# A new hand-written order of calls where the mLSTM ends and attention and the output projection begin, in a two-layer hybrid encoder on one core

## The chip, the cores and the metric

The kernel runs on one core of one Trainium2 chip, in one launch. The metric is the time of the launch on the device in microseconds (us), and the runs shown are executions of the same program. TensorE is PE in the profile (PEld its weight loads), VectorE is DVE, ScalarE is ACT, GpSimd is POOL, SyncE is SP.

## The reference, cut to what matters

Two sequences, of 256 and of 1024 tokens with 1024 features, go through the same two layers, in float32.

```
h = rmsnorm(x)
aq ak av | sz sxbc sdt | mq mk mv mo mi mf = split(h @ w_in)
ya = window attention (4 query heads, 2 key heads, blocks of 128, neighbours on each side, a sink)
yb = bidirectional SSD scan, gated with silu(z), normed
yc = bidirectional mLSTM, normed, gated with sigmoid(o)
x  = x + concat(ya, yb, yc) @ w_out
x  = x + expert-choice mixture of 16 experts(rmsnorm(x))
```

The window attention of a block is `p = exp(s - m)`, divided by `sum(p) + exp(sink - m)`, times V.

## The kernel before

Both sequences lie side by side as NC = 10 chunks of 128 tokens: 0 and 1 are the short sequence, 2 to 9 the long one. A layer has stages: norm and transposes, input projection with the convolutions, SSD, mLSTM, attention with output projection, routing, and the experts. Attention and output projection take the chunks in the order 2 to 9, 0, 1, and a chunk's number n there is its place in this order. Layers are a loop, so each line runs twice.

Nothing plans the work at run time: each engine has its own list of calls, written out by hand, does them strictly in that order, and waits in front of a call until counters (semaphores) of other engines have come far enough. A call that waits holds up all that stands behind it on its engine. A helper adds one to its own engine's counter after each instruction and waits for it, so instructions of DVE, ACT and POOL run one by one. Because helpers record them, most rows carry a helper's line: L1472 is `mm` (any matmul), L976 a tensor_tensor of DVE, L980, L982 and L985 other forms of DVE. A float32 matmul is two instructions in the trace, a transpose one.

The calls that matter here, with n the chunk's place (of the mLSTM calls the chunk itself):

- PE: `ml_sum(9)` is the last product of the mLSTM. `turn_qk(n)` transposes normed queries and keys (3 transposes), `scores(n, j)` makes the scores of half the heads, `turn_p(n, h)` transposes the probabilities of head h, `turn_y(n, 0)`, `(n, 1)` transpose the outputs of SSD and mLSTM, and `turn_y(n, 2)` multiplies probabilities and V. `out_proj(n, hf, i0, i1)` does steps i0 to i1 of the 8 contraction steps of one half of the output columns; one step is 2 instructions of 512 columns. Steps 0 to 3 need `keep_y(n, 0)`, 4 and 5 `keep_y(n, 1)`, 6 and 7 `keep_y(n, 2)`.
- DVE: `ml_read(c)` takes the mLSTM sums from PSUM, `ml_output(c)` makes its output and the sums of squares (10 instructions, the last one lets POOL make the root), `ml_gate(c)` scales and gates it when POOL has made the root. `attn_square(n)` sums the squares of queries and keys. `keep_turned(n)` takes the result of `turn_qk(n)` from PSUM (counter `a_kept`). `attn_shift(n, j)` adds the bias to scores and takes the maximum; its second half (j = 1) releases ACT's exponentials. `attn_den(n)` makes one over the sum of the exponentials and releases `attn_scale(n)`. `keep_y(n, j)` takes the result of `turn_y(n, j)` from PSUM. `add_x` adds the residual, `take_x(0)` is the first of them.
- POOL: `rroot` is the root for a norm (2 instructions), `attn_root(n)` the same for queries and keys, `attn_norm(n)` scales queries and keys (2 instructions), `attn_scale(n)` divides all probabilities of a block.
- ACT: `attn_exps(0)`, `attn_exps(1)`, `keep_p(0)`, `keep_p(1)`, `attn_exps(2)`, in this order, then norm, `keep_p` and `attn_exps` of each next block. `keep_p(n)` copies what `turn_p(n, h)` left in PSUM.

The waits at the head of the calls that the change moves past each other:

```
turn_p(n, h):    pn_made >= n + 1          (attn_scale(n) done), p_kept two heads back
turn_y(n, 2):    p_kept >= 4 * (n + 1), yt_copied >= 3 * n + 2, and for n < 2 a_kept >= n + 4
scores(n, j):    a_kept >= turned_for(n), and for n >= 1 s_read >= 2 * n + j
out_proj:        yt_copied >= 3 * n + 1, + 2, + 3 at steps 0, 4, 6
attn_scale(n):   r_made >= n + 1           (attn_den(n) done)
attn_den(n):     sink_exp >= n + 1         (attn_exps(n) done)
```

After the calls named in the diff, `for n in range(1, NC + 1)` on PE (and its like on the others) goes through the other blocks in a fixed weave, which begins with `out_proj(1, 0, 0, 1)`, `turn_qk(5)`, `out_proj(1, 0, 1, 2)`, `scores(3, 0)`, `out_proj(1, 0, 2, 3)`, `turn_p(2, 0)`.

Of the kernel before, what the change touches and what calls it, by code (L numbers as in the profile page):

```python
# [9 lines left out]
NC = T // P  # L10
# [30 lines left out]
UNITS = []  # L41
# [65 lines left out]
def program(nc, wi, wo, wga, wup, wdn, par, cst, onehot, xp, xs_in, yp, ys, btab, h2p, h2s, flip):  # L107
# [4 lines left out]
    with ctx:  # L112
# [237 lines left out]
        proj_read = layer_sem("proj_read")  # L350
# [125 lines left out]
        with nc.Fori(0, DEPTH) as layer:  # L476
          with nc.Block() as block:
# [106 lines left out]
            def _(pool):  # L584
# [73 lines left out]
                def attn_root(n):  # L658
                    pool.wait_ge(a_squared, n + 1)
                    rroot(QKS[:, n, :], QKS[:, n, :], 6, 1.0 / HD, EPS, pool_chain)  # L660
# [13 lines left out]
                def attn_scale(n):  # L674

                    nk, c0 = attn_keys(ORDER[n])
                    pool.wait_ge(r_made, n + 1)
                    v = PSC[n % 2][:, :, 0:nk * P]
                    link(pool.tensor_tensor(v, v, ADEN[n % 2].unsqueeze(2).to_broadcast([P, AH, nk * P]), ALU.mult), pn_made)  # L679
# [3 lines left out]
                for c in range(NC + 1):  # L683
                    if c + 1 < NC:
                        ml_mask(c + 1, 0)
                        ml_mask(c + 1, 1)
                    if c == NC:
                        attn_norm(2)
                        attn_norm(3)
                        attn_scale(0)  # L690
                    if c >= 1:
                        pool.wait_ge(h_summed, c)
                        rroot(rsb, ssb, MH, 4.0 / HD, 4 * EPS, h_rooted)
                    if 1 <= c < NC - 1:
                        attn_root(c - 1)
                    if c in (3, 4):
                        attn_norm(c - 3)

                attn_norm(4)
                attn_scale(1)  # L700
                attn_root(NC - 2)
                attn_root(NC - 1)
                for n in range(NC + 1):
                    if n >= 1:
                        pool.wait_ge(n2_squared, n)
# [266 lines left out]
            def _(dve):  # L972
# [271 lines left out]
                def keep_turned(n):  # L1244
                    dve.wait_ge(a_turned, n + 1)
                    c, b = ORDER[n], 3 if n < 3 else 2
                    ts(QT[:, :, c * P:(c + 1) * P], ps[:, b, 0:256].rearrange("p (j t) -> p j t", j=2), pr("qg"), HD ** -0.5,
                       ALU.mult, ALU.mult)
                    ts(KT[:, c * P:(c + 1) * P], ps[:, b, 256:384], pr("kg"), None, ALU.mult, to=a_kept)
# [35 lines left out]
                for c in range(NC):  # L1285
                    if c >= 1:
                        ml_read(c - 1)
                    if c >= 2:
                        ml_gate(c - 2)
                    if c == NC - 1:  # L1290
                        keep_turned(0)
                        keep_y(0, 0)
                    if c >= 1:
                        ml_output(c - 1)
                    if 1 <= c < NC - 1:
                        attn_square(c - 1)
                    if c + 1 < NC:
                        ml_weights(c + 1)
# [4 lines left out]
                attn_shift(0, 1)  # L1303
                keep_turned(2)
                ml_gate(NC - 2)
                keep_y(0, 1)
                attn_shift(1, 0)
                attn_den(0)
                attn_shift(1, 1)
                keep_turned(3)  # L1310
                ml_output(NC - 1)
                attn_den(1)
                attn_square(NC - 2)
                attn_square(NC - 1)
                attn_shift(2, 0)
                keep_y(0, 2)
                ml_gate(NC - 1)
                attn_shift(2, 1)

                def add_x(c, hf):  # L1320
                    dve.wait_ge(op_made, 2 * c + hf + 1)
# [32 lines left out]
                def take_x(n):  # L1354
                    dve.wait_ge([xo_loaded0, xo_loaded1][n % 2], 16 * (n // 2 + 1))
                    add_x(n, 0)

                keep_y(1, 0)
                take_x(0)
                keep_y(1, 1)  # L1360
                attn_den(2)
                keep_turned(4)
                keep_y(1, 2)
                for n in range(1, NC - 1):
                    add_x(n - 1, 1)
                    if n + 4 < NC:
# [101 lines left out]
            def _(pe):  # L1468
# [360 lines left out]

                turn_qk(1)  # L1830
                pe.wait_ge(wo_loaded, 32)
                out_proj(0, 0, 0, 4)
                pe.wait_ge(proj_read, len(UNITS))
                out_proj(0, 1, 0, 1)
                pe.wait_ge(nd_read, 2 * NC)
                scores(0, 0)
                scores(0, 1)
                turn_qk(2)
                out_proj(0, 1, 1, 4)
                turn_y(0, 1)  # L1840
                scores(1, 0)
                pe.wait_ge(wo_loaded_late, 32)
                out_proj(0, 0, 4, 6)
                scores(1, 1)
# [1 line left out]
                out_proj(0, 1, 4, 6)  # L1846
                for h in range(AH):
                    turn_p(0, h)
                scores(2, 0)
                turn_y(0, 2)  # L1850
                scores(2, 1)
                turn_y(1, 0)
                out_proj(0, 0, 6, 8)
                turn_p(1, 0)
                turn_p(1, 1)
                out_proj(0, 1, 6, 8)
                turn_y(1, 1)
                turn_p(1, 2)
                turn_p(1, 3)
                turn_qk(4)  # L1860
                turn_y(1, 2)
                for n in range(1, NC + 1):
                    out_proj(n, 0, 0, 1)
                    if n + 4 < NC:
                        turn_qk(n + 4)
                    out_proj(n, 0, 1, 2)
                    if n + 2 < NC:
                        scores(n + 2, 0)
                    out_proj(n, 0, 2, 3)
                    if n + 1 < NC:  # L1870
                        turn_p(n + 1, 0)
                    out_proj(n, 0, 3, 4)
                    if n + 1 < NC:
                        turn_p(n + 1, 1)
                    out_proj(n, 0, 4, 5)
                    if n + 2 < NC:
                        scores(n + 2, 1)
                    turn_h2(n - 1, 0)
                    out_proj(n, 0, 5, 6)
                    if n + 1 < NC:  # L1880
                        turn_y(n + 1, 0)
                        turn_p(n + 1, 2)
                    out_proj(n, 0, 6, 7)
                    if n + 1 < NC:
                        turn_p(n + 1, 3)
                    out_proj(n, 0, 7, 8)
                    turn_h2(n - 1, 1)
                    out_proj(n, 1, 0, 1)
                    if n + 1 < NC:
                        turn_y(n + 1, 1)  # L1890
                    out_proj(n, 1, 1, 3)
                    if n + 1 < NC:
                        turn_y(n + 1, 2)
                    out_proj(n, 1, 3, 4)
                    logits(n - 1)
                    out_proj(n, 1, 4, 8)
                    if n == NC - 2:
                        pe.wait_ge(aff_made, NC - NP)
                        for j in range(4):
                            last = pe.transpose(ps[0:2 * E, 7, j * P:(j + 1) * P], AFTM[:, j, 0:2 * E], ident)  # L1900
                        last.then_inc(aff_turned, 1)
# [149 lines left out]
```

## Time and profile before

| | |
|---|---|
| median of 3 runs | 2626.4 us (2625.22 to 2630.47) |
| the profiled execution, its own time | 2630.47 us |
| its span in the trace | 2628.8 us |
| what lies around the span | 1.7 us |
| PE busy | 2444.2 us (93%) |
| DVE, ACT, POOL busy | 1063.2, 555.9, 529.1 us |
| granted TensorE clock, mean | 0.96 |

The profiled execution is also the slowest of the three, 4.1 us above the median. The change lies in two short stretches, one in each layer, at about 580 to 640 us and 1885 to 1945 us of the span.

### The profile page before, as it was taken

What the parts mean: (1) busy time and instruction counts of PE and PEld (TensorE: products, weight loads), DVE (VectorE), ACT (ScalarE), POOL (GpSimd) and SP (SyncE); (2) the same over time, 40 slices, a digit from 0 to 9 for tenths busy, and PEclk for the clock granted to TensorE, in tenths of its full rate; (3) what the DMA queues carried; (4) which work ended last, traced back from release to release, by engine and by line L of the source; (5) the groups of instructions that cost most, each with busy time, mean ns of one, the idle gap of its engine ahead of it and who ended that gap; (6) DMA issues with size and microseconds to landing.
All of it is one profiled execution on the core that took longest, in us unless ns stands there. A gap on an engine that the chain in (4) does not pass through costs nothing. (4 is left out here: it accounts for less than half of the span.)

```text
span 2628.8 us, 34275 instructions
## 1 busy us (share of the span) xinstructions
PE 2444.2 (93%) x13486; PEld 1771.9 (67%) x13486; DVE 1063.2 (40%) x2134; ACT 555.9 (21%) x1194; POOL 529.1 (20%) x544
## 2 busy tenths in 40 slices
PE   5999999998995999999869999999989959999997
PEld 3567577884553788788635675878745537878876
DVE  3762355595437211111138514445854371111111
ACT  3220222233330011111132202323333300111110
POOL 1002443143110111111110114432331101112111
PEclk8999999999997999999989999999989979999999
DMA  6010222111126588887431011311212266878782
GB/s 213 18 33 17 96 80 81 57 66 71 63 80 227 169 289 274 281 288 251 113 118 35 17 65 64 97 49 65 81 49 72 73 224 208 283 265 297 258 282 72
DMA packets 149656, 357.63 MB, mean 136 GB/s; under 512 B 9981, under 2 KB 38273, under 8 KB 149410
## 3 DMA queue, kind: packets, MB, share of 16 engines
q1 hardware_dynamic: 134514, 313.42, 33.4%
q0 software_dynamic: 14976, 41.95, 6.4%
q8 instruction: 110, 1.80, 0.3%
q14 instruction: 56, 0.46, 0.1%
HBM read 313.06 MB, written 47.52 MB: 137 GB/s over the span
## 5 line engine op out<-in xcount | busy, mean ns | idle before, releaser
L1472 PE MATMUL ps<-MID,HT 128*128 128x512 f32 (+1 forms) x2176 | 598.1, 497 | 4.3 <-PE ps L1472 3.1
L1472 PE MATMUL ps<-HT,MID 128*128 128x160 f32 (+1 forms) x4192 | 583.8, 307 | 8.1 <-DVE HT L976 3.8
L1472 PEld LDWEIGHTS ps<-HT,MID 128*128 128x128 f32 (+1 forms) x4192 | 563.0, 189 | 26.7 <-issue 26.4
L1472 PE MATMUL ps<-RING,HT 128*128 128x256 f32 (+2 forms) x2080 | 482.2, 401 | 7.0 <-ACT SCR L863 2.2
L1472 PEld LDWEIGHTS ps<-RING,HT 128*128 128x128 f32 (+1 forms) x2080 | 382.0, 195 | 97.8 <-issue 41.4
L1472 PEld LDWEIGHTS ps<-MID,HT 128*128 128x128 f32 (+1 forms) x2176 | 232.7, 153 | 227.2 <-issue 210.7
L1472 PE MATMUL ps<-HT,RING 128*128 128x512 f32 (+1 forms) x960 | 354.3, 526 | 2.1 <-ACT MID L786 1.5
L985 DVE SCALAR_TENSOR_TENSOR HT<-HT,ps 128x160 f32<-128x160 f32 x128 | 41.2, 322 | 711.8 <-ACT HT L962 711.8
L1472 PEld LDWEIGHTS ps<-HT,RING 128*128 128x128 f32 x960 | 180.9, 191 | 163.3 <-issue 155.7
L742 POOL DMA_INDIRECT y_sample<-SCR,idxs x32 | 50.6, 1581 | 741.3 <-ACT SCR L969 741.3
L976 DVE TENSOR_TENSOR HT<-ps,part 128x512 f32<-128x512 f32 (+1 forms) x220 | 141.5, 643 | 121.2 <-PE ps L1810 51.7
L962 ACT ACTIVATE HT<-ps 128x160 f32<-128x160 f32 x128 | 38.9, 304 | 605.1 <-PE ps L1472 605.1
L1472 PE MATMUL ps<-MID 128*64 128x128 f32 (+3 forms) x1136 | 138.5, 319 | 13.6 <-DVE RING L980 9.9
L1472 PEld LDWEIGHTS ps<-MID 64*128 64x128 f32 (+1 forms) x1136 | 105.5, 181 | 53.5 <-issue 38.4
L610 POOL TENSOR_TENSOR SCR<-MID,small 128x512 f32<-128x512 f32 x32 | 39.7, 1242 | 345.9 <-DVE MID L976 272.8
L976 DVE TENSOR_TENSOR SCR<-SCR,ps 128x512 f32<-128x512 f32 x80 | 55.0, 687 | 122.6 <-POOL SCR L624 98.8
L976 DVE TENSOR_TENSOR SCR<-SCR,small 128x1024 f32<-128x1024 f32 (+1 forms) x60 | 59.3, 988 | 95.3 <-POOL SCR L619 94.6
L679 POOL TENSOR_TENSOR SCR<-SCR,small 128x1536 f32<-128x1536 f32 (+1 forms) x20 | 48.1, 2405 | 194.1 <-DVE small L1272 194.0
L967 ACT ACTIVATE SCR<-ps,small 128x512 f32<-128x512 f32 x64 | 44.0, 687 | 201.6 <-PE ps L1472 201.6
L1472 PE MATMUL ps<-MID,SCR 128*128 128x65 f32 (+1 forms) x640 | 81.3, 281 | 4.6 <-DVE TMP L976 4.5
L976 DVE TENSOR_TENSOR TMP<-MID,small 128x256 f32<-128x256 f32 (+1 forms) x64 | 27.0, 421 | 143.0 <-PE ps L1472 141.9
L903 ACT ACTIVATE SCR<-SCR,small 128x128 f32<-128x128 f32 x160 | 64.3, 402 | 89.7 <-POOL SCR L655 85.0
(217 smaller groups left out, 2188.2 us busy)
## 6 DMA issues: line engine op xcount, KB each, us to landing
MID<-w_gate SPq DMA_DIRECT2D x32, 2048.0 KB, 8.6
MID<-w_up SPq DMA_DIRECT2D x32, 2048.0 KB, 14.2
MID<-w_down SPq DMA_DIRECT2D x32, 2048.0 KB, 14.7
RING<-w_in SPq DMA_DIRECT2D x22, 1024.0 KB, 5.3
SCR<-cs_rows SPq DMA_DIRECT2D x20, 1024.0 KB, 5.2
SCR<-m_rows SPq DMA_DIRECT2D x20, 512.0 KB, 3.7
MID<-y_sample SPq DMA_DIRECT2D x16, 512.0 KB, 7.8
MID<-w_out SPq DMA_DIRECT2D x8, 1024.0 KB, 6.5
```

What stands on the lines that cost most here:

```text
L610: link(pool.tensor_tensor(DXS[:, n % 2, d, :].rearrange("p (h e) -> p h e", h=SH), XS[:, c, :].rearrange("p (h e) -> p h e", h=SH), WS[:, ...
L679: link(pool.tensor_tensor(v, v, ADEN[n % 2].unsqueeze(2).to_broadcast([P, AH, nk * P]), ALU.mult), pn_made)
L742: pool.indirect_dma_start(ys[:, :], bass.IndirectOffsetOnAxis(ap=idxs[:, e:e + 1], axis=0), YO[e % 2], None, compute_op=ALU.add, bounds_ch ...
L903: link(act.activation(v, v, ACT.Exp, bias=U[:, c, d, h:h + 1], scale=-1.0), md_exp if h == MH - 1 else act_chain)
L962: link(act.activation(THG, ps[:, 2 + f % 2, 0:TOK], ACT.Tanh, scale=0.5), gate_tanh)
L967: link(act.mul(YO[e % 2][:, hf * 512:(hf + 1) * 512], ps[:, 4 + hf, :], gts[:, e:e + 1]), down_scaled)
L976: link(dve.tensor_tensor(out, a, b, op), to)
L985: link(dve.scalar_tensor_tensor(out=out, in0=a, scalar=x, in1=b, op0=op0, op1=op1), to)
L1472: return pe.matmul(out, a, b, start=start, stop=stop)
```

## The change

No instruction is added or taken away. Calls stand in another order on three of the four engines; ACT's order stays.

```diff
 POOL, end of the mLSTM loop and behind it
                         attn_norm(2)
                         attn_norm(3)
-                        attn_scale(0)
                     if c >= 1:
                         pool.wait_ge(h_summed, c)
                         rroot(rsb, ssb, MH, 4.0 / HD, 4 * EPS, h_rooted)
-                    if 1 <= c < NC - 1:
+                    if 1 <= c < NC:
                         attn_root(c - 1)
...
+                attn_scale(0)
                 attn_norm(4)
+                attn_root(NC - 1)
                 attn_scale(1)
-                attn_root(NC - 2)
-                attn_root(NC - 1)

 DVE, in the last turn of the mLSTM loop and behind it
                     if c == NC - 1:
                         keep_turned(0)
+                    if c >= 1:
+                        ml_output(c - 1)
+                    if c == NC - 1:
                         keep_y(0, 0)
                     if c >= 1:
-                        ml_output(c - 1)
-                    if 1 <= c < NC - 1:
                         attn_square(c - 1)
...
                 ml_gate(NC - 2)
+                attn_shift(1, 0)
                 keep_y(0, 1)
-                attn_shift(1, 0)
+                attn_shift(1, 1)
+                ml_output(NC - 1)
                 attn_den(0)
-                attn_shift(1, 1)
                 keep_turned(3)
-                ml_output(NC - 1)
+                attn_square(NC - 1)
+                ml_gate(NC - 1)
                 attn_den(1)
-                attn_square(NC - 2)
-                attn_square(NC - 1)
-                attn_shift(2, 0)
-                keep_y(0, 2)
-                ml_gate(NC - 1)
-                attn_shift(2, 1)
...
+                keep_y(0, 2)
                 keep_y(1, 0)
                 take_x(0)
                 keep_y(1, 1)
+                keep_turned(4)
+                attn_shift(2, 0)
+                attn_shift(2, 1)
+                keep_y(1, 2)
                 attn_den(2)
-                keep_turned(4)
-                keep_y(1, 2)

 PE, behind the mLSTM loop
                 turn_qk(1)
                 pe.wait_ge(wo_loaded, 32)
-                out_proj(0, 0, 0, 4)
-                pe.wait_ge(proj_read, len(UNITS))
-                out_proj(0, 1, 0, 1)
+                out_proj(0, 0, 0, 2)
                 pe.wait_ge(nd_read, 2 * NC)
                 scores(0, 0)
                 scores(0, 1)
+                out_proj(0, 0, 2, 4)
                 turn_qk(2)
-                out_proj(0, 1, 1, 4)
+                pe.wait_ge(proj_read, len(UNITS))
+                out_proj(0, 1, 0, 3)
+                scores(1, 0)
+                out_proj(0, 1, 3, 4)
                 turn_y(0, 1)
-                scores(1, 0)
                 pe.wait_ge(wo_loaded_late, 32)
                 out_proj(0, 0, 4, 6)
                 scores(1, 1)
...
                 for h in range(AH):
                     turn_p(0, h)
-                scores(2, 0)
                 turn_y(0, 2)
-                scores(2, 1)
-                turn_y(1, 0)
-                out_proj(0, 0, 6, 8)
                 turn_p(1, 0)
                 turn_p(1, 1)
+                out_proj(0, 0, 6, 8)
+                turn_y(1, 0)
                 out_proj(0, 1, 6, 8)
                 turn_y(1, 1)
                 turn_p(1, 2)
                 turn_p(1, 3)
                 turn_qk(4)
+                scores(2, 0)
                 turn_y(1, 2)
+                scores(2, 1)
```

## Rows read from the trace of the kernel before

**Rows 1.** Busy time by window: length, PE, PEld, DVE, ACT, POOL, granted clock, DMA share, GB/s.

```profile
628.00:800.00 172.00, 170.73 (x814) 93.64 (x813) 72.33 (x153) 54.16 (x135) 26.68 (x31) 1.00 0.20 74
```

**Rows 2.** Timeline of PE, layer 1: start, duration, instruction, idle before with its releaser.

```profile
585.49 0.55 PE L1731 MATMUL ps<-cstt,RING 128*128 128x128 f32 x3
585.87 4.46 PE L1472 MATMUL ps<-MID,HT 128*128 128x512 f32 x10
590.26 1.13 PE L1472 MATMUL ps<-RING,HT 64*128 64x256 f32 x8
...
598.64 0.92 PE L1472 MATMUL ps<-RING,HT 64*128 64x384 f32 x4
...
605.82 1.09 PE L1753 MATMUL ps<-cstt,SCR 128*128 128x128 f32 x4 [3.63 <-ACT MID L931]
...
614.10 0.82 PE L1753 MATMUL ps<-cstt,SCR 128*128 128x128 f32 x6
...
622.99 2.83 PE L1472 MATMUL ps<-MID 128*64 128x128 f32 x24 [4.94 <-DVE RING L980]
626.12 1.18 PE L1472 MATMUL ps<-MID,HT 128*128 128x512 f32 x2 [0.30 <-PE ps L1472]
...
630.23 0.49 PE L1753 MATMUL ps<-cstt,SCR 128*128 128x128 f32 x3
```

**Rows 3.** Timeline of DVE, layer 1.

```profile
583.30 0.69 DVE L976 TENSOR_TENSOR HT<-ps,part 128x512 f32<-128x512 f32 x1
...
589.72 0.35 DVE L980 TENSOR_SCALAR RING<-ps,part 128x128 f32<-128x128 f32 x1
...
599.67 0.96 DVE L976 TENSOR_TENSOR SCR<-ps,bias 128x768 f32<-128x768 f32 x1 [0.68 <-PE ps L1472]
...
602.05 0.48 DVE L982 TENSOR_SCALAR HT<-ps,part 128x256 f32<-128x256 f32 x1
...
602.96 0.17 DVE L985 SCALAR_TENSOR_TENSOR small<-TMP 128x4 f32<-128x4 f32 x1
...
606.28 0.16 DVE L976 TENSOR_TENSOR small<-small 128x4 f32<-128x4 f32 x1
...
606.69 0.60 DVE L976 TENSOR_TENSOR TMP<-MID 128x384 f32<-128x384 f32 x1
...
607.91 0.88 DVE L976 TENSOR_TENSOR TMP<-MID 128x384 f32<-128x384 f32 x1
...
621.57 0.16 DVE L976 TENSOR_TENSOR small<-small 128x4 f32<-128x4 f32 x1 [4.18 <-ACT small L923]
```

**Rows 4.** Timeline of POOL, layer 1.

```profile
599.14 1.89 POOL L679 TENSOR_TENSOR SCR<-SCR,small 128x1024 f32<-128x1024 f32 x1 [8.04 <-DVE small L1272]
...
607.77 0.61 POOL L666 TENSOR_TENSOR RING<-MID,SCR 128x256 f32<-128x256 f32 x1
...
609.13 2.75 POOL L679 TENSOR_TENSOR SCR<-SCR,small 128x1536 f32<-128x1536 f32 x1
...
614.00 0.20 POOL L589 TENSOR_SCALAR SCR<-SCR 128x6 f32<-128x6 f32 x1
...
615.68 0.62 POOL L666 TENSOR_TENSOR RING<-MID,SCR 128x256 f32<-128x256 f32 x1
```

**Rows 5.** Timeline of ACT, layer 1: the first instruction of attn_exps(2).

```profile
618.30 0.61 ACT L922 ACTIVATE SCR<-SCR,small 128x384 f32<-128x384 f32 x1
```

**Rows 6.** Timeline of DVE, layer 2: keep_y(0, 0).

```profile
1888.70 0.69 DVE L976 TENSOR_TENSOR HT<-ps,part 128x512 f32<-128x512 f32 x1
```

**Rows 7.** Timeline of PE, layer 2: five projection steps, and turn_p(2, 0).

```profile
1892.12 6.41 PE L1472 MATMUL ps<-MID,HT 128*128 128x512 f32 x10
...
1939.75 0.49 PE L1753 MATMUL ps<-cstt,SCR 128*128 128x128 f32 x3
```

**Rows 8.** Busy time by window, with the granted clock third from the end.

```profile
602.00:612.00 10.00, 5.25 (x31) 2.77 (x30) 9.24 (x23) 4.53 (x13) 5.19 (x6) 0.83 0.01 2
...
1886.00:1898.00 12.00, 11.29 (x48) 7.44 (x46) 8.71 (x23) 0.79 (x2) 3.23 (x6) 0.72 0.45 159
```

## The prediction, made before the changed kernel was run

> **What bounds the kernel now.** I read the busy table first (TensorE 93%), then busy time by window, then the timelines of the four engines side by side, once per layer. The window of the woven blocks that follow the change shows TensorE busy for 170.7 of 172 us at full clock [rows 1]: there is no slack there in which a late start could be made good, so a microsecond lost or won ahead of it, in the hand-over from mLSTM to attention, is one at the end. The hand-over itself is not bound by TensorE. Its timeline has a wait of 3.63 us in the middle of the four `turn_p(0, h)` and one of 4.94 us ahead of `turn_y(1, 2)` [rows 2]. The first is for ACT: `keep_p(0)` stands behind `attn_exps(1)`. The second is for `keep_turned(4)`, which on VectorE stands behind `attn_den(2)`, which waits 4.18 us for the exponentials [rows 3]. The reader should see that both are chains of short calls on VectorE, ACT and GpSimd with TensorE waiting at their end. So the question is not how much work is moved but when each link of these chains now gets its turn. I lay the new order out call by call, in layer 1, with durations from the rows; I take starts to the next start, so the hand-off is inside.
>
> **Step 1, up to scores(0, 0).** VectorE is the busy engine here. Before, it goes from `keep_y(0, 0)` at 583.30 to the end of `keep_turned(1)` at 590.07 [rows 3]. The new order puts `attn_square(8)` into that run: 607.91 - 606.69 = 1.22 us [rows 3]. So `keep_turned(1)` ends at 591.3 and scores(0, 0) start at 591.4 instead of 590.26 [rows 2]. Ahead of them TensorE did five projection steps, 0.88 us each (590.26 - 585.87 over 5). Now it does two, and these begin late as well: `ml_output(8)` (602.96 to 606.44, 3.5 us with its last instruction) goes ahead of `keep_y(0, 0)`, which ends at 583.30 + 3.3 + 0.7 = 587.3 where it was 584.0. TensorE waits from 585.9 to 587.4, works 1.8 us, and waits again from 589.2 to 591.4: 3.7 us that were work before.
>
> **Step 2, up to the first probabilities.** From scores(0, 0) TensorE has both scores (1.1), two steps (1.8), `turn_qk(2)` (585.87 - 585.49 = 0.38), three steps (2.6): 5.8 us, scores(1, 0) at 597.2. From the start of scores to VectorE's start on them are 1.03 us (598.64 to 599.67) [rows 2, 3]; `attn_shift(1, 0)` takes 2.0 (602.05 - 599.67 = 2.38 for a second half, less two small instructions of 0.2). Only then comes `keep_y(0, 1)` (256 columns, under the 0.69 of 512; I take 0.45), so steps 4 and 5 start at 600.7 and scores(1, 1) at 602.5. VectorE stands at `attn_shift(1, 1)` until 603.5 and ends it at 605.9. Here is the new long wait: `attn_den(0)`, which was done at 599.0 (it releases the scale at 599.14 [rows 4]), now stands behind `ml_output(9)`, and on GpSimd `attn_scale(0)` stands behind the root that `ml_output(9)` releases. So: `ml_output(9)` to 605.9 + 3.5 = 609.4, root 1.33 (606.44 to 607.77 [rows 3, 4]) to 610.7, scale 1.89 [rows 4] to 612.6, TensorE's first `turn_p(0, 0)` at 612.7. TensorE has done all that stands ahead at 602.5 + 0.9 + 0.4 + 1.8 = 605.6. It waits 7.1 us, in place of the 3.63 us, which go: ACT has ended `attn_exps(1)` by then (released at 605.9, 3.2 us long, 609.1) and copies at once.
>
> **Step 3, the second block.** The four heads of block 0 go at ACT's pace and are covered by GpSimd's chain, which sets the next start: `attn_norm(4)` 1.36 (607.77 to 609.13), `attn_root(9)` 1.68 (614.00 to 615.68), `attn_scale(1)` 2.75 [rows 4], with hand-offs 6.0 us, so `turn_p(1, 0)` starts at 618.7. From there TensorE has four `turn_p` (1.3; six transposes are 0.7, from 614.10 with 0.82 less the overlap with the next), four steps (3.5) and six transposes of `turn_y` (0.7): `turn_qk(4)` at 624.2. VectorE answers with `keep_turned(4)` 1.5 us after its start (0.55, and 602.96 - 602.05 = 0.9), which the scores cover but for 0.3; `turn_y(1, 2)` starts at 625.8 and needs 3.13 us (626.12 - 622.99). The 4.94 us wait is gone, as the order intends. Scores(2, 1) start at 628.9.
>
> **Step 4, what is late next.** scores(2, 1) used to come ahead of block 1's work; now the whole chain to the probabilities of block 2 hangs behind them: 1.03 to VectorE, 2.38 for the shift (632.3), 3.3 for the exponentials (618.30 to 621.57 [rows 3, 5]), 0.4 for `attn_den(2)`, 2.75 and hand-offs for the scale: 639.0 is the start of `turn_p(2, 0)`. On TensorE the weave reaches that call after waiting some 2 us at `turn_qk(5)` (it wants `keep_y(1, 2)`, behind the shift) and some 3 us here. Before, the call starts at 630.23 [rows 2]. This is 8.8 us later in layer 1. The norm of block 0, which starts on ACT only after `attn_den(2)` too, I cost at nothing: three projection steps and a score of TensorE (3.5 us) lie between `turn_p(2, 0)` and the call that needs it, and it is ready about a microsecond before; were it later, each microsecond would count in full. After it the lists agree, and by [rows 1] nothing is recovered.
>
> **Step 5, layer 2.** The same lists run, so the new start lies by the same distance behind `keep_y(0, 0)` of before: 1888.70 - 583.30 = 1305.4, 639.0 + 1305.4 = 1944.4, against 1939.75 [rows 6, 7]: 4.6 us. It is less because this execution's layer 2 had a slow piece of its own: five steps took 6.41 us instead of 4.46 at a mean clock of 0.72 [rows 2, 7, 8], and VectorE's chain hides that in the new order. The median run is 4.1 us below the profiled one; I take it that this piece is most of that, and that a usual layer 2 loses 8.8 as well.
>
> **The clock.** [...] The new order has a longer wait (7.1 us) and work right behind `turn_p(1, 0)` that nothing covers. I take 1.8 us per layer, half of 3.4, and keep 0 and 6.8 (two such stretches, as there are two groups of long waits) as ends. [...]
>
> **The sum.** Against the profiled execution: 2630.5 + 8.8 + 4.6 + 3.6 = 2647.5. Against the median: 2626.4 + 2 x 8.8 + 3.6 = 2647.6. I forecast 2647.
>
> **Rivals.**
> - *The old waits go and nothing comes in their place.* 3.63 + 4.94 = 8.6 us per layer, 2609. It speaks for it that both releasers are really moved out of the way. It decides if `turn_p(0, 0)` can start before about 606 us, thus if `attn_den(0)` is not held by `ml_output(9)`; VectorE works strictly in order, so I see no way, unless scores(1, 1) come 7 us earlier than I have them. 0.08.
> - *Old and new waits balance.* The new wait would have to be some 3 us shorter and the tail absorbed: 2626. 0.05.
> - *The tail of step 4 is absorbed.* If the exponentials of block 2 were ready in time (no waits at `turn_qk(5)` and `turn_p(2, 0)`, together 5.3 us per layer), 2647 - 10.6 = 2636. Rows 1 speak against it for what follows, but these waits rest on my longest chain. 0.12.
> - *The clock falls twice per layer,* by the sum's upper end: 2626.4 + 17.6 + 2 x 6.8 is 2657.6; with partial cover 2654 to 2657. The second short of work between two waits in step 4 speaks for it; against it, the waits of step 4 are of 2 and 3 us, shorter than the two of before. 0.15. [...]
>
> **How the numbers follow.** The forecast has 0.60, from 2643 (no clock loss) to 2652. The range takes in the absorbed tail below and most of the clock rival above: 2636 to 2656, which leaves out the two first rivals and the last corner of the clock, under 0.2. Within 0.2% is 5.3 us to either side, about what a measurement of this kernel can tell from no change. Faster 0.08, same 0.05, slower 0.87.
>
> **What would show it.** In the new trace: TensorE's waits of 3.63 and 4.94 us gone; a wait of about 7 us ahead of `turn_p(0, 0)`, released by GpSimd's scale; VectorE idle by some 3 us ahead of `attn_shift(1, 1)`; waits of 1.5 and 2.2 us around the first two projection steps, of about 2 ahead of `turn_p(1, 0)`, of 2 and 3 us at `turn_qk(5)` and `turn_p(2, 0)`; the same pattern in both layers; busy time of each engine unchanged but for the clock. Step 2 is wrong if the scale starts before 609 us, step 4 if `turn_p(2, 0)` comes without a wait. The forecast as a whole fails if the woven blocks of the new trace begin no later than before.

## The result, and the profile after

The changed kernel takes 2644.7 us (median of 4 runs, 2642.46 to 2651.67) against 2626.7 us before (4 runs): a ratio of 1.0070, 95% interval 1.0049 to 1.0093, 18 us slower. A second set of runs (e10 below) gave 2645.7 against 2624.0 us, a ratio of 1.0089 (1.0069 to 1.0109). The forecast was 2647 us in a range of 2636 to 2656. The profiled execution, which is not among the four, was a long one again, 2654.3 us of its own time with a span of 2652.6; so I compare the hand-over by its length in the trace, and whole kernels by the ratio.

Busy time hardly moves (page of the profile; before, the table above):

```profile
PE 2458.6 (93%) x13486; PEld 1776.2 (67%) x13486; DVE 1063.5 (40%) x2134; ACT 556.0 (21%) x1194; POOL 527.8 (20%) x544
```

The same instructions run, and TensorE's are 14 us longer in sum, as its granted clock is lower (0.955 on the mean against 0.960). Only some 6 us of them lie in the two hand-overs (busy 41.0 us before and 47.0 after in layer 1, 46.6 and 47.0 in layer 2). Some 8 lie ahead of the first one, where the clock is 0.95 on the mean instead of 0.97; in the second profile of the changed kernel (e10) it is 0.97 there too, so these do not belong to the change. What is new is when the instructions run. TensorE's waits in the hand-over of layer 1, 585 to 645 us (sum, times, longest):

```profile
PE ps L1752 <- POOL SCR L679: 8.2, 2, 7.3
PE ps L1471 <- DVE HT L975: 2.8, 2, 1.4
PE ps L1471 <- DVE RING L979: 2.3, 2, 2.0
PE ps L1730 <- DVE HT L975: 2.0, 1, 2.0
```

Lines are one smaller than before. The two waits of [rows 2] (3.63 for ACT, 4.94 for `keep_turned(4)`) are gone; the largest is now 7.3 us for line 679, GpSimd's `attn_scale(0)`. The timeline of TensorE in layer 1 shows the order of it:

```profile
588.39 0.63 PE L1764 MATMUL ps<-cstt,MID 128*128 128x128 f32 x4 [0.30 <-PE ps L1471]
...
594.53 1.96 PE L1471 MATMUL ps<-MID,HT 128*128 128x512 f32 x4 [1.43 <-DVE HT L975]
598.46 1.54 PE L1471 MATMUL ps<-RING,HT 64*128 64x256 f32 x8 [1.98 <-DVE RING L979]
...
609.58 1.96 PE L1471 MATMUL ps<-MID,HT 128*128 128x512 f32 x4 [1.40 <-DVE HT L975]
...
621.87 1.11 PE L1752 MATMUL ps<-cstt,SCR 128*128 128x128 f32 x4 [7.29 <-POOL SCR L679]
...
627.67 1.54 PE L1752 MATMUL ps<-cstt,SCR 128*128 128x128 f32 x6 [0.93 <-POOL SCR L679]
629.01 3.62 PE L1471 MATMUL ps<-MID,HT 128*128 128x512 f32 x4
...
637.66 1.53 PE L1471 MATMUL ps<-MID 128*64 128x128 f32 x24 [0.28 <-DVE RING L979]
639.50 0.92 PE L1471 MATMUL ps<-RING,HT 64*128 64x384 f32 x4 [0.30 <-PE ps L1471]
...
643.47 0.87 PE L1730 MATMUL ps<-cstt,RING 128*128 128x128 f32 x3 [2.00 <-DVE HT L975]
...
649.55 0.55 PE L1752 MATMUL ps<-cstt,SCR 128*128 128x128 f32 x3 [1.19 <-POOL SCR L679]
```

From the top: `turn_y(0, 0)`, with which I let the hand-over begin; the two first projection steps; scores(0, 0); steps 4 and 5; `turn_p(0, 0)` behind the long wait; `turn_p(1, 0)`; two steps that take 3.62 us (granted clock 0.50 from 627 to 633 us) where two take 1.88 at full clock (at 612.70 in the same trace, 1.00 from 612.5 to 615); `turn_y(1, 2)`; scores(2, 1); `turn_qk(5)`; `turn_p(2, 0)`. VectorE's timeline has the idle time that goes with the long wait, at `attn_shift(1, 1)`, and then `attn_den(0)`, behind `ml_output(9)`; below it GpSimd's `attn_scale(0)`:

```profile
612.50 0.96 DVE L975 TENSOR_TENSOR SCR<-ps,bias 128x768 f32<-128x768 f32 x1 [3.06 <-PE ps L1471]
...
618.19 0.16 DVE L975 TENSOR_TENSOR small<-small 128x4 f32<-128x4 f32 x1
```

```profile
619.68 2.14 POOL L679 TENSOR_TENSOR SCR<-SCR,small 128x1024 f32<-128x1024 f32 x1
```

The clock in this stretch is 0.57 on the mean (busy time by window, columns as in [rows 8]):

```profile
618.00:634.00 16.00, 10.50 (x40) 6.64 (x41) 5.91 (x13) 2.55 (x7) 9.75 (x10) 0.57 0.00 1
```

From `turn_y(0, 0)` to `turn_h2(0, 0)`, the first call of the steady weave that needs the norm, the hand-over is 52.2 us long before and 64.5 after in layer 1, 57.8 and 64.5 in layer 2: 12.3 and 6.8 us, 19 of the profiled pair's 24 us. The rest comes from other stages: `turn_y(0, 0)` of layer 1 already comes at 588.39 instead of 581.33, 7 us late, and about 2 of these are made good between the layers. That does not belong to the change, since in e10, the same kernel, this call comes at 579.48.

### The profile page after: what moved, and what is told of

It reads as the page before. It is cut to its first block, busy times and chain, and to the rows that moved or that the text cites. A ratio compares the mean times of both kernels' runs of the same rounds, so it can differ in the third digit from the quotient of the medians.

```text
span 2652.6 us, 34275 instructions
## 1 busy us (share of the span) xinstructions
PE 2458.6 (93%) x13486; PEld 1776.2 (67%) x13486; DVE 1063.5 (40%) x2134; ACT 556.0 (21%) x1194; POOL 527.8 (20%) x544
## 4 chain that ended last, share of the span: by engine, by line
PE 38%; DVE 7%; POOL 2%; issue 1%; ACT 1%; DMA 1%; SPq 0%; POOLq 0%; DVEq 0%; ACTq 0%
PE ps L1471 36%; DVE SCR L975 1%; DVE TMP L975 1%; POOL SCR L619 1%; PE ps L1935 1%; POOL SCR L624 1%; PE ps L1752 0%; DVE HT L975 0%; DVE TMP L984 0%; DVE MID L1093 0%; DVE idxus L1342 0%; PE ps L1809 0%; DVE TMP L1341 0%; DVE TMP L1344 0%; DVE MID L975 0%
## 5 line engine op out<-in xcount | busy, mean ns | idle before, releaser
L1471 PEld LDWEIGHTS ps<-RING,HT 128*128 128x128 f32 (+1 forms) x2080 | 384.8, 197 | 103.3 <-issue 47.1
```

The costliest lines, as they stand in the source:

```text
L1471: return pe.matmul(out, a, b, start=start, stop=stop)
```

## The experiments

Each of e1 to e12 is compared with the kernel before on the same chip. "Length" is from `turn_y(0, 0)` to `turn_h2(0, 0)` in layers 1 and 2 of the profiled execution.

| kernel | us | ratio, 95% interval | length |
|---|---|---|---|
| before (first profile) | 2626.7 | 1 | 52.2, 57.8 |
| changed | 2644.7 | 1.0070 (1.0049 to 1.0093) | 64.5, 64.5 |
| e10, changed again | 2645.7 | 1.0089 (1.0069 to 1.0109) | 63.6, 63.2 |
| e1, changed, den(0) back | 2643.8 | 1.0068 (1.0054 to 1.0082) | 63.4, 62.7 |
| e4, changed, scores(2) back | 2630.3 | 1.0024 (1.0013 to 1.0034) | 55.1, 57.0 |
| e5, changed, one wait filled | 2645.3 | 1.0077 (1.0063 to 1.0090) | 64.5, 64.9 |
| e9, changed, all waits filled | 2642.4 | 1.0064 (1.0043 to 1.0084) | 62.0, 61.5 |
| e2, before, den(0) late | 2629.5 | 1.0026 (1.0016 to 1.0036) | 57.9, 56.4 |
| e6, before, step 1 | 2635.5 | 1.0045 (1.0031 to 1.0059) | 57.7, 57.6 |
| e3, before, turned(4) first | 2613.5 | 0.9949 (0.9934 to 0.9964) | 47.4, 49.0 |
| e12, e3 again | 2614.4 | 0.9961 (0.9946 to 0.9976) | 48.2, 47.1 |
| e7, e3 and keep_p(0) first | 2617.1 | 0.9974 (0.9961 to 0.9987) | 49.4, 49.9 |
| e8, e7 and ml_output(9) late | 2612.7 | 0.9955 (0.9937 to 0.9972) | 46.2, 49.3 |
| e11, e3, squares late, filled | 2619.0 | 0.9969 (0.9956 to 0.9982) | 48.4, 48.5 |

### e1: the long wait taken out of the changed kernel

```diff
 DVE
                 keep_y(0, 1)
+                attn_den(0)
                 attn_shift(1, 1)
                 ml_output(NC - 1)
-                attn_den(0)
 POOL
                         attn_norm(3)
+                        attn_scale(0)
...
-                attn_scale(0)
                 attn_norm(4)
```

> The changed kernel with attn_den(0) back ahead of attn_shift(1, 1) on VectorE, and attn_scale(0) back ahead of the root for ml_output(9) on GpSimd. Theory of the prediction (each link's turn decides): the wait of 7.3 us ahead of turn_p(0, 0) goes, but ACT then makes turn_p(0, 2) wait about 3.5 us as before, and the next start, turn_p(1, 0), still hangs on ml_output(9), root, attn_norm(4), attn_root(9), attn_scale(1), one scale (1.9 to 2.1 us) and a hand-off earlier: about 2.4 us per layer less than the changed kernel, 2640 us. Rival (the 7.3 us wait is the loss): its removal gives back 3.7 us per layer beyond the old 3.63, and the clock loss with it, 5 to 7 us per layer, 2631 to 2635.

Neither. The wait of 7.3 us is gone and 3.63 us for ACT are back, as in both theories, and the next start is again GpSimd's scale. TensorE's timeline of e1, layer 1:

```profile
612.05 0.81 PE L1752 MATMUL ps<-cstt,SCR 128*128 128x128 f32 x4 [3.63 <-ACT MID L930]
...
619.00 1.54 PE L1752 MATMUL ps<-cstt,SCR 128*128 128x128 f32 x6 [3.65 <-POOL SCR L679]
...
640.16 0.90 PE L1752 MATMUL ps<-cstt,SCR 128*128 128x128 f32 x3 [2.80 <-POOL SCR L679]
640.85 1.91 PE L1471 MATMUL ps<-MID,HT 128*128 128x512 f32 x2
```

`turn_p(1, 0)` comes 37.2 us after `turn_y(0, 0)` (at 581.80 here) and came 39.3 after it in the changed kernel: 2.1 us, about as expected, and at `turn_p(2, 0)` it is 2.8 us (58.4 against 61.2). Then 1.7 us of them go back: behind this call, where the wait was 2.80 us instead of 1.19, TensorE works at a lower clock (0.57 on the mean at 640 to 644 us; 1.00 at 649 to 652 in the changed kernel), and the step takes 1.91 us instead of 1.02. In the whole kernel no difference is clear: the interval of 1.0068 overlaps both intervals of the changed kernel (1.0070 and 1.0089). The longest wait of the profile, 7.3 us, was worth 0.2 to 1.9 us per layer by the lengths, against the two profiles of the changed kernel. Where it was taken away, another took most of its place (GpSimd's chain from `ml_output(9)`, 3.65 us in place of 0.93).

### e5 and e9: what the clock costs

Matmuls of 384 columns whose result nobody reads fill waits of TensorE; `keep_clock(b, n)` does n of them into PSUM bank b: ten ahead of `turn_p(0, 0)` in e5; in e9 three more ahead of `turn_p(1, 0)`, three ahead of `turn_qk(5)` and four ahead of `turn_p(2, 0)`.

```diff
 PE, e5
+                keep_clock(6, 10)
                 for h in range(AH):
                     turn_p(0, h)
 PE, e9 in addition
                 turn_y(0, 2)
+                keep_clock(3, 3)
                 turn_p(1, 0)
...
                     out_proj(n, 0, 0, 1)
+                    if n == 1:
+                        keep_clock(3, 3)
                     if n + 4 < NC:
                         turn_qk(n + 4)
...
+                    if n == 1:
+                        keep_clock(3, 4)
                     if n + 1 < NC:
                         turn_p(n + 1, 0)
```

> The changed kernel with ten matmuls of 384 columns, whose result nobody reads, put on TensorE where it waits 7.3 us ahead of turn_p(0, 0); they fill about 6.4 us of that wait. Theory (the granted clock is half for some 12 us after that wait and doubles what nothing covers behind turn_p(1, 0): 1.54 for 0.82, 3.62 for 1.88, 0.98 for 0.63): 2.6 us per layer less, 2639 to 2640, and a clock of 1.00 from 620 to 632 us. Rival (the clock falls in the short waits too, or the loss is covered): within 1 us per layer, 2643 to 2645.

> The kernel of e5 with fillers in the later waits too: three matmuls of 384 columns ahead of turn_p(1, 0), three ahead of turn_qk(5) and four ahead of turn_p(2, 0), once each per layer. Theory (with the first wait filled, the clock fell in these and took 1.2 us before turn_qk(4) and 1.3 us behind turn_p(2, 0)): clock 1.00 throughout, 2.5 us per layer less than e5, a ratio to the kernel before of 1.0050 to 1.0060. Rival (the clock costs nothing that counts): as e5 and the changed kernel, 1.007 to 1.008.

e5 missed what its theory asked for, and went with its rival. The long wait was filled, but the clock fell in the next ones (0.57 on the mean at 620 to 624 us, 0.62 at 641 to 645). TensorE's timeline of e5: the wait ahead of `turn_p(1, 0)` and the projection steps behind it, 2.57 us for 1.88, then the wait at `turn_p(2, 0)` and its step, 1.92 us for 1.02:

```profile
620.81 1.54 PE L1752 MATMUL ps<-cstt,SCR 128*128 128x128 f32 x6 [2.34 <-POOL SCR L679]
622.14 2.57 PE L1471 MATMUL ps<-MID,HT 128*128 128x512 f32 x4
...
641.29 0.90 PE L1752 MATMUL ps<-cstt,SCR 128*128 128x128 f32 x3 [2.80 <-POOL SCR L679]
641.99 1.92 PE L1471 MATMUL ps<-MID,HT 128*128 128x512 f32 x2
```

With every wait filled (e9) the clock is 1.00 where it is 0.73 in the changed kernel beside it (e10); first the window of e9, then that of e10:

```profile
612.00:650.00 38.00, 35.20 (x164) 19.02 (x163) 20.77 (x44) 12.74 (x31) 14.27 (x15) 1.00 0.09 32
```

```profile
605.00:643.00 38.00, 25.88 (x112) 13.69 (x112) 18.98 (x39) 12.52 (x31) 14.27 (x15) 0.73 0.05 19
```

From `turn_p(0, 0)` to `turn_h2(0, 0)` e9 takes 28.4 us (619.95 to 648.31), e10 31.3 (611.72 to 643.05), and layer 2 is alike: the clock costs 3.0 us per layer there (2.7 against the first profile, 621.87 to 652.92). The whole length shows 1.6 against e10, since in e9 the scores of block 0 met a slow stretch that e10 did not have (2.08 us for 1.13; 0.67 on the mean at 590 to 600 us in e9, 1.00 at 590 to 595 in e10), and 2.5 and 3.1 against the first profile. The lengths are 2.5 and 3.4 us under those of e5, as the theory said; the ratio of 1.0064 lies between the theory (1.0050 to 1.0060) and the rival (1.007 to 1.008) and its interval holds both. What stays over the kernel before, 8.4 us per layer by the ratio, is waiting, and the lower clock around scores(0, 0) (0.72 on the mean at 590 to 602 us), which e9 does not fill.

### e2 and e6: parts of the change, put alone on the kernel before

e2 moves `attn_den(0)` behind `ml_output(9)` and `attn_scale(0)` on GpSimd behind the root for it, as the change does. e6 has the first part alone.

```diff
 DVE, e2
                 attn_shift(1, 0)
-                attn_den(0)
                 attn_shift(1, 1)
                 keep_turned(3)
                 ml_output(NC - 1)
+                attn_den(0)
                 attn_den(1)
 PE, e6 (with the change's edits to the last turn of the mLSTM loop on DVE and POOL)
-                out_proj(0, 0, 0, 4)
-                pe.wait_ge(proj_read, len(UNITS))
-                out_proj(0, 1, 0, 1)
+                out_proj(0, 0, 0, 2)
                 pe.wait_ge(nd_read, 2 * NC)
                 scores(0, 0)
                 scores(0, 1)
+                out_proj(0, 0, 2, 4)
                 turn_qk(2)
-                out_proj(0, 1, 1, 4)
+                pe.wait_ge(proj_read, len(UNITS))
+                out_proj(0, 1, 0, 4)
```

> The kernel before with only attn_den(0) moved behind ml_output(9) on VectorE and attn_scale(0) behind the root for it on GpSimd. Theory: turn_p(0, 0) starts at about 609.8 instead of 601.6, after a wait of 8 us, but ACT is free by then, the exponentials of block 2 start about 3 us later than before, and some half-clock work is added: 3 to 5 us per layer, 2633 to 2637. Rival (all of the new wait is lost): 8.2 less 3.6 us and two clock stretches, 6 to 8 us per layer, 2639 to 2643.

> The kernel before with only the first part of the change: ml_output(8) ahead of keep_y(0, 0), attn_square(8) inside the last turn of the mLSTM loop (its root on GpSimd with it), and two projection steps instead of five ahead of scores(0, 0). Theory: scores(0, 0) start 1.1 us later, scores(1, 0) 3 us later, attn_shift(1, 1) 2.3 us later, of which the missing attn_square(8) further down gives 1.2 back: 1.1 to 2.3 us per layer, 2629 to 2631. Rival (the 3.7 us of TensorE's waits in step 1 are all lost): 2634.

e2: the wait is 7.95 us long, as expected, and costs 5.4 us in all by the medians, 2.7 per layer (3.4 by the ratio), at the low edge of 3 to 5:

```profile
609.46 1.11 PE L1753 MATMUL ps<-cstt,SCR 128*128 128x128 f32 x4 [7.95 <-POOL SCR L679]
```

e6 missed, and on the rival's side: 11.5 us, 5.8 per layer, where I expected 1.1 to 2.3 and the rival 3.7. I had given back the 1.2 us of the square that VectorE no longer does further down. But nothing there waits for VectorE's sum of work; each link hangs on the one before. scores(1, 1) start 21.1 us after `turn_y(0, 0)` instead of 17.3 and ACT's copies (24.5 before) 28.3 after it, 3.8 later both:

```profile
603.46 0.92 PE L1471 MATMUL ps<-RING,HT 64*128 64x384 f32 x4
...
610.64 1.09 PE L1752 MATMUL ps<-cstt,SCR 128*128 128x128 f32 x4 [3.63 <-ACT MID L930]
```

All that TensorE did not do ahead of scores(0, 0) was missing later. The rest, to 5.4 in layer 1, is work at a lower clock further down (0.50 at 611 to 617 and at 628 to 633 us): `turn_y(0, 2)`, scores(2, 1) and the first step behind `turn_y(1, 2)` take 5.63 us together, where the kernel before took 3.57, and a shorter wait covers a part of it.

### e3 and e4: the good move, and the bad one beside it

e3 is the kernel before with two calls moved; e4 the changed kernel with scores(2, ·) and their shifts back at their old places.

```diff
 DVE, e3
                 keep_y(1, 1)
-                attn_den(2)
                 keep_turned(4)
                 keep_y(1, 2)
+                attn_den(2)
 PE, e4
                     turn_p(0, h)
+                scores(2, 0)
                 turn_y(0, 2)
+                scores(2, 1)
...
                 turn_qk(4)
-                scores(2, 0)
                 turn_y(1, 2)
-                scores(2, 1)
 DVE, e4
                 attn_den(1)
+                attn_shift(2, 0)
...
                 keep_y(0, 2)
+                attn_shift(2, 1)
                 keep_y(1, 0)
                 take_x(0)
                 keep_y(1, 1)
                 keep_turned(4)
-                attn_shift(2, 0)
-                attn_shift(2, 1)
                 keep_y(1, 2)
```

> The kernel before with only keep_turned(4) and keep_y(1, 2) moved ahead of attn_den(2) on VectorE. Theory: the wait of 4.94 us ahead of turn_y(1, 2) goes and the half clock behind it, while attn_den(2) and attn_scale(2) keep their times, so turn_p(2, 0) starts at 625.0 instead of 630.2: 5.3 us per layer, 2616 us. Rival (attn_scale(2) is made late by the calls put ahead of attn_den(2), and a wait for it takes the place): within 1 us per layer, 2625 to 2627.

> The changed kernel with scores(2, 0) back ahead of turn_y(0, 2), scores(2, 1) behind it, and attn_shift(2, 0), attn_shift(2, 1) on VectorE behind attn_den(1) and keep_y(0, 2); keep_turned(4) and keep_y(1, 2) stay ahead of attn_den(2). Theory: the waits of 2.0 us at turn_qk(5) and 1.2 us at turn_p(2, 0) with the clock drop behind them are the price of step 4, 5.3 to 6.2 us per layer come back, 2632 to 2634. Rival (the tail is absorbed, the price is all in steps 1 to 3): within 1 us per layer of the changed kernel, 2643 to 2646.

Both theories hold, e4 with a somewhat larger gain than expected. In e3 the wait of 4.94 us is 1.13 and `turn_y(1, 2)` takes 1.53 us (clock 1.00 at 615 to 625 us) where [rows 2] has 2.83 (0.50 at 622.9 to 626):

```profile
622.06 1.53 PE L1472 MATMUL ps<-MID 128*64 128x128 f32 x24 [1.13 <-DVE RING L980]
```

e3 is 11.5 us faster than the kernel before (e12: 11.8), 5.7 per layer where 5.3 was expected. e4 is 5.3 us slower than before; between it and the changed kernel lie 1.0070 or 1.0089 less 1.0024, 12 to 17 us, 6 to 8.5 per layer, against 5.3 to 6.2 expected.

The parts add up: e6 + 11.5, e2 + 5.4, e3 - 11.5 make + 5.4, and e4, which has these three and the smaller moves of the change (`attn_shift(1, 0)` ahead of `keep_y(0, 1)`, `out_proj(0, 0, 6, 8)` and `turn_y(1, 0)` behind `turn_p(1, 1)`, and others), measures + 5.3. Each of these has an interval of 3 to 4 us to either side, so that they meet to 0.1 us is luck, and what the smaller moves do alone was not tried. The later scores(2, ·) make the rest.

### e7, e8, e11: is there more to win?

The diffs show the edits to ACT and VectorE. GpSimd's list is changed to match in e8 (`attn_root(8)` ahead of `attn_scale(1)`, the root for `ml_output(9)` behind `attn_norm(5)`) and in e11 (both roots behind `attn_norm(6)`), and on TensorE e8 has `out_proj(0, 1, 6, 8)` ahead of `turn_p(1, 0)`. e12 is e3 and e10 the changed kernel, both run again.

```diff
 ACT, e7 (on e3) and e8
                 attn_exps(0)
-                attn_exps(1)
                 keep_p(0)
+                attn_exps(1)
 DVE, e8 in addition
-                ml_gate(NC - 2)
                 keep_y(0, 1)
+                ml_gate(NC - 2)
...
                 keep_turned(3)
-                ml_output(NC - 1)
-                attn_den(1)
                 attn_square(NC - 2)
                 attn_square(NC - 1)
                 attn_shift(2, 0)
                 keep_y(0, 2)
-                ml_gate(NC - 1)
+                attn_den(1)
                 attn_shift(2, 1)
...
                 keep_turned(4)
+                ml_output(NC - 1)
                 keep_y(1, 2)
                 attn_den(2)
+                ml_gate(NC - 1)
 DVE, e11 (on e3, with keep_clock(3, 5) between turn_p(0, 1) and turn_p(0, 2))
-                attn_square(NC - 2)
-                attn_square(NC - 1)
                 attn_shift(2, 0)
...
                 keep_y(1, 1)
+                attn_square(NC - 2)
                 keep_turned(4)
+                attn_square(NC - 1)
                 keep_y(1, 2)
```

> The kernel of e3 (keep_turned(4) and keep_y(1, 2) ahead of attn_den(2)), and on ACT keep_p(0) ahead of attn_exps(1). Theory (VectorE's list sets the pace between 596 and 616 us, with no idle time between 602 and 616): the wait of 3.63 us in turn_p(0, h) falls below 1 us and comes back ahead of scores(2, 1), which need attn_shift(2, 0) at 609.4; within 1 us per layer of e3. Rival (each wait on TensorE is worth its length): 3 us per layer less than e3, a ratio to the kernel before of 0.9925 or below.

> The kernel of e7, and the work that nothing waits for soon is put later: ml_output(9) and ml_gate(9) behind keep_turned(4) and attn_den(2), both squares ahead of attn_shift(2, 0), the root of ml_output(9) on GpSimd behind attn_norm(5), out_proj(0, 1, 6, 8) ahead of turn_p(1, 0). Theory: attn_shift(2, 0) starts at 605 instead of 609.4, attn_scale(1) ends at 610 instead of 611.9, turn_p(2, 0) starts at 620 to 621.5 against 625.0 of e3: 3.5 to 5 us per layer less than e3, a ratio to the kernel before of 0.991 to 0.993. Rival (attn_scale(2) or the late ml_gate(9) takes the place): as e3, 0.995 to 0.996.

> The kernel of e3, with attn_square(8) behind keep_y(1, 1) and attn_square(9) behind keep_turned(4), their roots on GpSimd behind attn_norm(6), and five matmuls of 384 columns, whose result nobody reads, in the wait of 3.63 us between turn_p(0, 1) and turn_p(0, 2). Theory: VectorE's list ahead of attn_shift(2, 0) is 2.4 us shorter and TensorE keeps full clock, so that scores(2, 1) start 2.6 us earlier: 2 to 2.5 us per layer less than e3, a ratio to the kernel before 0.0015 to 0.002 below that of e3. Rival (another link, attn_scale(1) or keep_turned(4), ends no earlier): as e3.

> The kernel of e3 again, beside e11: a ratio to the kernel before of 0.995, and 47.4 to 49.0 us from turn_y(0, 0) to turn_h2(0, 0).

> The changed kernel again, beside the others on one chip, with a second profile: a ratio to the kernel before of 1.007, and from turn_y(0, 0) to turn_h2(0, 0) 64.5 us in both layers as in the first profile.

e7: the wait of 3.63 us falls to 0.39 and comes back, larger, ahead of scores(2, 1), which wait for `attn_shift(2, 0)` on VectorE. The timeline of TensorE:

```profile
600.28 0.81 PE L1753 MATMUL ps<-cstt,SCR 128*128 128x128 f32 x4 [0.39 <-ACT MID L931]
...
608.91 1.65 PE L1472 MATMUL ps<-RING,HT 64*128 64x384 f32 x4 [5.95 <-DVE SCR L976]
```

One long wait in place of a middling one, and a slower stretch behind it (0.69 on the mean at 608 to 615 us): the lengths are 49.4 and 49.9 against 47.1 to 49.0, on the mean 1.5 to 2.0 us more than e3, where within 1 us was expected. The rival is refuted: nothing was won. e8 takes that wait to 1.33 us and is about where e3 is, as its rival had it, not the 3.5 to 5 us per layer ahead of it. In layer 1 `turn_p(2, 0)` comes 41.3 us after `turn_y(0, 0)`, against 44.1 in e3, but 1.6 of these 2.8 us go again before `turn_h2(0, 0)`, 0.86 of them in a wait for VectorE; in layer 2 four steps take 5.03 us instead of 3.60 (clock 0.73 on the mean at 1905 to 1911 us). A likely reason for VectorE being late is `ml_gate(9)`, which now meets `attn_scale(2)` of GpSimd; first VectorE, then GpSimd in e8:

```profile
622.48 3.00 DVE L979 TENSOR_TENSOR SCR<-SCR,small 128x256 f32<-128x256 f32 x1 [0.68 <-POOL small L590]
```

```profile
622.45 2.75 POOL L679 TENSOR_TENSOR SCR<-SCR,small 128x1536 f32<-128x1536 f32 x1
```

The same instruction takes 0.42 us alone (at 571.92 us in the kernel before). e11 missed too, and went with its rival: it brought scores(2, 1) forward, but its `ml_gate(9)` meets `attn_scale(1)` (1.95 and 0.72 us for 0.42 and 0.42) and `turn_y(1, 2)` waits longer (1.57 us for 1.13) and runs at a lower clock (2.83 us for 1.53, 0.50 at 620 to 623 us); 48.4 and 48.5 us, no gain over e3 beside it (0.9969 against 0.9961). So e3, one line moved, is as fast as anything tried: e8, with many more moves, is level with it (0.9955 against 0.9949 and 0.9961), and nothing on top of it paid.

e10 and e12 show how far a repetition lies from its first run: the lengths of the changed kernel came out 1 us shorter than the 64.5 expected and its ratio 0.0019 higher, those of e3 within 1 us on the mean.

## Why the prediction was right

Point by point, in layer 1, with the times shifted by 7.06 us (`keep_turned(0)` starts at 582.40 before and 589.46 after):

- *Step 1* held to a tenth: scores(0, 0) at 591.4 + 7.06 = 598.46, and 598.46 in the trace; the waits around the first two steps are 1.43 and 1.98 (1.5 and 2.2 forecast). I had not seen that the clock falls in them (0.66 on the mean at 598 to 603 us): the two steps behind scores(0, 0) take 3.23 us, and scores(1, 0) come 1.7 us late.
- *Step 2* held: 3.06 us of idle time ahead of `attn_shift(1, 1)` (3), a wait of 7.29 us ahead of `turn_p(0, 0)` (7.1), released by the scale. All of it comes about 2 us later than laid out, mostly by what the clock took in step 1.
- *Step 3*: `turn_p(1, 0)` 5.80 us after `turn_p(0, 0)` (6.0). The wait ahead of it is 0.93 us, not 2, as TensorE's work before it ran at a lower clock (0.50 at 621 to 627 us); at full clock (e5, 1.00 at 612 to 620) it is 2.34. `turn_y(1, 2)` I took at 3.13 us from a row that had run at a clock of 0.50; here it needed 1.84 to the next start. That was 1.3 us too much, and the clock took more back: from `turn_p(1, 0)` to `turn_y(1, 2)` are 9.99 us, where 7.1 were forecast.
- *Step 4*: scores(2, 1) to `turn_p(2, 0)` 10.05 us (10.1), a wait of 2.00 at `turn_qk(5)` (2). At `turn_p(2, 0)` 1.19 instead of 3, because TensorE came slower; when it comes at full clock (1.00 at 624 to 640 us in e5, at 630 to 640 in e1) the wait is 2.80.
- *Step 5*: layer 2 has the same waits to 0.02 us. Its extra is 6.8 us by length (4.6 plus 1.8 forecast), as the slow piece of the profile before was hidden.
- *The clock* is the term that was too small. I took 1.8 us per layer from a range of 0 to 6.8. No run shows the 1.8 or the 6.8 as a price; both are my estimates, from the 3.4 us that I let one slow stretch cost at most: by [rows 8] 12 us at 0.72 on the mean are 6.7 us at 0.50 and the rest at 1.00, and half of 6.7 is 3.4. The trace of the kernel before does have a clock of 0.50 from 1889.3 to 1895.9 us, 6.6 us, and from 605.8 to 609.2, 3.4 us, right behind the wait of 3.63, but not what they cost. For the changed kernel the runs show this: e9 against e10 measures 3.0 behind `turn_p(0, 0)` (2.7 against the first profile). The slow work ahead of it is outside that figure. In layer 1 the sum was 8.8 + 1.8 = 10.6 and the length grew by 12.3. The clock came out dearer and `turn_y(1, 2)` cheaper than forecast; that these two misses partly cancel is luck.

Against the medians the forecast was 2.3 us too high (1.3 in the second set), within what single executions differ by. A slip that changed nothing: with no clock loss the sum is 2626.4 + 17.6 = 2644, not 2643.

Of the rivals, the absorbed tail is refuted by e4, and that the old waits go and nothing comes in their place by the changed kernel itself, though e3 shows that half of that rival was real: moved alone, `keep_turned(4)` does win its 5.7 us per layer. The clock that falls twice per layer is what the traces show (behind the waits of 1.98, 7.29 and 2.00 us in the first profile, 0.66, 0.50 and 0.57 on the mean: three times), at less than its full price; that other waits cover part of it is argued, not measured.

Where my reading was thinner than the sum suggests: I wrote of the 7.3 us as the long wait that costs. e1 and e2 show that it is worth 0.2 to 3.4 us per layer. The larger prices are the work not done ahead of scores(0, 0) (e6, 5.8) and the late scores(2, ·) (e4, 6 to 8.5), less what `keep_turned(4)` wins (5.7). The total was right because the chain was laid out call by call, with some luck between its terms, not because the longest wait was the cause. Which rows of clock loss belong to which wait in the changed kernel stays open beyond e9's 3.0 us; it varied between two profiles of one kernel (64.5 and 63.4 us on the mean).

## What to carry to other kernels

With hand-written lists, lay the new order out call by call over all engines: for each link ask what stands ahead of it now, and follow the chain to the next call of the busy engine; the length of a wait in the profile is not its price, since the next link may take its place (here, removing 7.3 us was worth about one, 3.63 us nothing, 4.94 us all and more). Look for a call that somebody waits for and that stands behind one which itself waits (here `keep_turned(4)` behind `attn_den(2)`): moving it alone gained as much as any larger reordering that was tried. When a duration is taken from a row, look at the clock of that row first.

## What the runs showed of the hardware

TensorE's clock fell behind waits of 1.4 to 2.0 us that stood near each other (0.66 on the mean at 598 to 603 us and 0.57 at 643 to 647 us in the changed kernel), and filling the longest wait alone left a drop at the next one (0.57 at 620 to 624 us in e5). But such waits are neither needed nor enough. In the kernel before the clock was 0.50 at 1890 to 1895 us with TensorE busy all the time, behind a wait of 0.71 us at 1887 (the slow steps of [rows 7]). From 500 to 579 us, ahead of the hand-over, it was 0.87 in the changed kernel and 0.96 in e10, the same kernel, both times with TensorE busy for 98% or more. And behind the wait of 2.00 us at `turn_qk(5)` it stayed up in layer 1 of e1 and e5 (1.00 at 634 to 640 us in e1; in e5 the step behind it takes 1.02 us). So which wait brings a drop is not shown; shown is that with all waits from `turn_p(0, 0)` on filled the clock was 1.00 (e9).

Behind the waits of 7.29 and 7.30 us of the changed kernel it was 0.50 in each layer anew (at 621 to 627 us and at 1936 to 1941 us).

Operations of VectorE that read two operands from SBUF and started while GpSimd ran `attn_scale` ended only after it: 3.00 us instead of 0.42 for 256 columns in e8, 0.28 us behind the end of `attn_scale(2)` and its 2.75 us; 1.95 instead of 0.42 in e11, 0.28 behind `attn_scale(1)`; 1.41 instead of 0.42 in the changed kernel (at 620.69 us), 0.28 behind `attn_scale(0)`; 1.76 instead of 0.56 for 384 columns in e2 (at 608.06 us), 0.42 behind it. `attn_shift`, which reads one operand from PSUM, was not held: in the changed kernel it takes its usual 0.96 us in the middle of `attn_scale(2)` (first VectorE, then GpSimd):

```profile
648.27 0.96 DVE L975 TENSOR_TENSOR SCR<-ps,bias 128x768 f32<-128x768 f32 x1
```

```profile
646.74 2.75 POOL L679 TENSOR_TENSOR SCR<-SCR,small 128x1536 f32<-128x1536 f32 x1 [17.95 <-DVE small L1271]
```

In e8 VectorE lost 2.58 us, nearly the whole length of GpSimd's instruction. An order that makes the two coincide can lose what it gained elsewhere; that this is all of e8's missing gain was not tried.
